# Second routed layer: experts ranked by load, run in pairs of 128 and 64 slots, steps of 1,024 columns

## What is computed

```python
D_MODEL, SEQ, TOP_K = 1024, 256, 2      # N_EXPERTS_2 = 8, D_FF_EXPERT = 3584
def moe_swiglu(x, w_router, w_gate, w_up, w_down):
    logits = (x @ w_router).astype(jnp.float32)
    top_val, top_idx = lax.top_k(logits, TOP_K)
    top_w = jax.nn.softmax(top_val, axis=-1)
    gate = jnp.einsum('bsk,bske->bse', top_w,
                      jax.nn.one_hot(top_idx, N_EXPERTS_2, dtype=jnp.float32)).astype(x.dtype)
    y = jnp.zeros_like(x)
    for e in range(N_EXPERTS_2):
        h = jax.nn.silu(x @ w_gate[e]) * (x @ w_up[e])
        y = y + gate[..., e:e + 1] * (h @ w_down[e])
    return y
```

## Time and profile before

| what | value |
|---|---|
| time, median of 3 runs (range) | 2262.71 us (2261.13 to 2263.49) |
| span of the profiled execution | 2253.2 us |
| TensorE matmul busy | 2128.2 us, 94% |
| TensorE weight load, VectorE, ScalarE busy | 76%, 69%, 57% |
| read from HBM over the span | 595.15 MB |

### The profile page before, as it was taken

The page is one execution under the profiler, slowest core; times in us unless marked ns, Lnnn a source line. Parts: engine busy times, 40 slices in busy tenths (PEclk is TensorE's granted clock), DMA queues, the critical chain, the costliest instruction groups (busy, mean ns, idle before and its releaser), DMA issues. The chain is left out here.

```text
span 2253.2 us, 33106 instructions
## 1 busy us (share of the span) xinstructions
PE 2128.2 (94%) x12230; PEld 1708.1 (76%) x12230; DVE 1550.7 (69%) x2214; ACT 1274.0 (57%) x1674; POOL 196.4 (9%) x148
## 2 busy tenths in 40 slices
PE   8998999998988989999998899999999999999996
PEld 8886884443787779997777688888888888888885
DVE  4557651221555686665367789888888888888887
ACT  4554441111334454443464777787777878777774
POOL 2112100000000113340001010101001010001000
PEclk9998999999989999999999899999999999999999
DMA  8640649999552245658212899999999999999994
GB/s 264 197 150 1 196 158 393 417 416 415 176 178 94 85 153 163 203 163 215 80 40 99 301 369 367 373 367 374 370 375 367 375 377 368 374 369 371 368 396 177
DMA packets 293952, 602.56 MB, mean 267 GB/s; under 512 B 17835, under 2 KB 123711, under 8 KB 285520
## 3 DMA queue, kind: packets, MB, share of 16 engines
q1 hardware_dynamic: 285392, 571.56, 70.2%
q0 software_dynamic: 8448, 29.49, 4.1%
HBM read 595.15 MB, written 5.83 MB: 267 GB/s over the span
## 5 line engine op out<-in xcount | busy, mean ns | idle before, releaser
L2139 ACT ACTIVATE arena_rounded<-ring 128x1024 fp32r<-128x1024 f32 x452 | 470.9, 1061 | 114.8 <-DMA ring<-in_moe_w_up_dram 67.0
L2856 DVE TENSOR_TENSOR ring_rounded<-ring,arena_rounded 128x1024 fp32r<-128x1024 f32 x452 | 525.0, 1218 | 13.1 <-ACT arena_rounded L2139 11.6
L1210 PE MATMUL psF<-arena_rounded 128*128 128x512 f32 x896 | 357.6, 399 | 1.6 <-ACT arena_rounded L2161 1.6
L1212 PE MATMUL psF<-arena_rounded 128*128 128x512 f32 x896 | 354.2, 395 | 0.0
L1211 PE MATMUL psF<-ring_rounded,arena_rounded 128*128 128x512 f32 x896 | 352.9, 394 | 0.0
L2413 DVE TENSOR_TENSOR ring_rounded<-ring,ring_rounded 128x2048 fp32r<-128x2048 f32 (+1 forms) x68 | 147.1, 2165 | 157.0 <-ACT ring_rounded L1965 156.8
L1212 PEld LDWEIGHTS psF<-arena_rounded 128*128 128x128 f32 x896 | 168.5, 188 | 39.2
L1210 PEld LDWEIGHTS psF<-arena_rounded 128*128 128x128 f32 x896 | 168.8, 188 | 38.9 <-ACT arena_rounded L2161 1.8
L1211 PEld LDWEIGHTS psF<-ring_rounded,arena_rounded 128*128 128x128 f32 x896 | 168.7, 188 | 37.8
L1211 PE MATMUL psB<-ring_rounded,PT_rounded 128*128 128x512 f32 x448 | 177.6, 396 | 0.0
L1965 ACT ACTIVATE ring_rounded<-ring 128x2048 fp32r<-128x2048 f32 (+1 forms) x71 | 128.6, 1813 | 84.7 <-PE psF L1212 62.7
(11 more groups left out here) (485 smaller groups left out, 4625.8 us busy)
## 6 DMA issues: line engine op xcount, KB each, us to landing
ring<-in_moe_w_gate_dram SPq DMA_DIRECT2D x224, 512.0 KB, 5.8
ring<-in_moe_w_up_dram SPq DMA_DIRECT2D x224, 512.0 KB, 5.7
ring<-in_moe_w_down_dram SPq DMA_DIRECT2D x224, 512.0 KB, 5.5
ring<-in_w_dram SPq DMA_DIRECT2D x48, 1024.0 KB, 16.7
arena<-in_w_dram SPq DMA_DIRECT2D x16, 1024.0 KB, 18.9
ring<-in_w_in_dram SPq DMA_DIRECT2D x14, 1024.0 KB, 5.3
ring<-in_ff_w_gate_dram SPq DMA_DIRECT2D x11, 1024.0 KB, 7.2
ring<-in_ff_w_up_dram SPq DMA_DIRECT2D x11, 1024.0 KB, 9.7
```

Of the source, the lines that this page charges most:

```text
L1210: mm(bank, x1, w1, start=start, stop=False, skip_group_check=open_groups)
L1212: return mm(bank, x2, w1, start=False, stop=stop, skip_group_check=open_groups)
L2139: ap_(half_slot(slot, w_hi).bitcast(R32), half_slot(slot, raw_halves), ACT.Copy).then_inc(q["high"], 1)
L2856: V.tensor_tensor(half_slot(slot, low_halves).bitcast(R32), half_slot(slot, raw_halves), half_slot(slot, w_hi), ALU.subtract).then_inc(q[" ...
```

## The change

The second routed layer is rewritten; the rest of the program stays.

1. **Order and slots.** The counts of all experts are summed on TensorE ("totals2"), and `sort_experts` on VectorE (some 26 small instructions and two of 128 x 896) ranks them: expert 0 stays first with 128 slots; the four with most tokens of the others take positions 1, 3, 5, 7 with 128 slots (`BIG`), the three with the fewest take positions 2, 4, 6 with 64 slots (`FEW`). SyncE reads the expert's number for a position from SBUF. If an expert had more tokens than slots, the old form of the layer would run as a second round.
2. **Steps.** Each expert has 4 steps: three of 1,024 columns (24 pieces of 512 KB: 8 gate, 8 up, 8 down) and one of 512 (12 pieces). Position 0 runs alone, then the pairs (1, 2), (3, 4), (5, 6) take turns step by step, then position 7 runs alone.
3. **The 128-slot experts** keep the products by halves. A step of 1,024 columns has three PSUM banks; the first four pieces of up are gone through twice, once for each half of the columns, the second time after the SiLU has freed a bank. Down pieces are loaded, rounded and subtracted two at a time (1 MB, 128 x 2,048).
4. **The 64-slot experts** multiply in plain float32 straight from the ring, with no high and low: a stationary block of 128 x 64, the two halves of the piece's columns into partitions 0 to 63 and 64 to 127 of one bank.
5. **Rows.** Gate and up pieces of a 1,024-column step have rows of 4 KB; a down load reads 8 KB per partition that lie together (16 KB rows of four, two at a time).
6. **The rest.** The rows of all seven later experts are numbered in one go; GpSimd brings and stores rows in a written-out order, 64 rows for the small ones. Semaphores of the old form get base values (`layer.wait`, `base`), so that the old form can still run after the new one.

The core of the diff ("..." marks what is left out):

```diff
+BIG = (0, 1, 3, 5, 7)
+FEW = 64
+HALF_SLOTS = 2 * RING
...
+class Step:
+
+
+    def __init__(self, t, pos, s, alone):
+        self.t, self.pos, self.s, self.alone = t, pos, s, alone
+        self.big, self.wide = pos in BIG, s < 3
+        self.first, self.last = s == 0, s == 3
+        self.base = 1024 * s
+        self.pieces = 8 if self.wide else 4
+        self.halves = 2 if self.big and self.wide else 1
+
...
+        for group in ((0,), (1, 2), (3, 4), (5, 6), (7,)):
+            for s in range(4):
+                for pos in group:
+                    self.steps.append(Step(len(self.steps), pos, s, len(group) == 1))
+        n = len(self.steps)
+        self.at, self.pieces, self.loads = {}, [], []
+        for t in range(n + 1):
+            for part, u in (("gate", t), ("up", t), ("down", t - 1)):
+                if not 0 <= u < n:
+                    continue
+                for j in range(self.steps[u].pieces):
+                    idx = len(self.pieces)
+                    self.at[u, part, j] = idx
+                    self.pieces.append(self.steps[u].big)
+                    if part != "down" or j % 2 == 0:
+                        self.loads.append((idx, u, part, j, 2 if part == "down" else 1))
+        self.big_no = list(itertools.accumulate(int(b) for b in self.pieces))
+        self.landed, self.count = {}, [0] * HALF_SLOTS
+        for idx, _, _, _, n_ in self.loads:
+            slot = idx % HALF_SLOTS
...
+            def load_sorted(layer):
...
+                for idx, t, part, j, n in order.loads:
+                    st = order.steps[t]
+                    if st.pos not in expert:
+                        if len(expert) == 1:
+                            sp.wait_ge(experts_sorted, 1)
+                        expert[st.pos] = nc.sync.value_load(expert_no[0:1, st.pos:st.pos + 1], min_val=0, max_val=E2 - 1)
...
+                    if idx >= HALF_SLOTS:
+                        sp.wait_ge(piece_used, idx + n - HALF_SLOTS)
...
+                    if part == "down":
+                        c = st.base // 512
+                        if st.wide or st.big:
+                            src = fours[e, c + j // 4, :, j % 4:j % 4 + 2, :]
+                        else:
+                            src = twos[e, c, j // 2, :, :, :]
+                        src = src.rearrange("e p f n -> p (e f) n")
+                    elif st.wide:
+                        src = (gates if part == "gate" else ups)[e, j // 2, :, j % 2, st.base:st.base + 1024]
+                        src = src.rearrange("e p n -> p e n")
+                    else:
+                        src = (gates if part == "gate" else ups)[e, j, :, :, st.base:st.base + 512]
+                        src = src.rearrange("e p a n -> p (e a) n")
...
+                def few_product(st, bank, part, j):
+
+                    w = few_piece(st.t, part, j, 1 if st.wide else 2)
+                    for a in range(1 if st.wide else 2):
+                        k = j if st.wide else 2 * j + a
+                        for b in range(2):
+                            n = 512 if st.wide else 256
+                            ins = mm(bank[FEW * b:FEW * b + FEW, 0:n], few_T[:, k, :], w[:, a, n * b:n * b + n],
+                                     start=(k == 0), stop=(k == KT - 1))
+                    ins.then_inc(piece_used, 1)
+
...
+                def gate(st):
+                    if st.first:
+                        if st.big:
+                            pe.wait_ge(x_low, order.halved_x[st.pos + 1])
+                        else:
+                            pe.wait_ge(x_high, order.turned_x[st.pos + 1])
...
+                        X = many_banks(st)
+                        hi, lo = big_piece(st.t, "gate", j, 1 if st.wide else 2)
+                        for b in range(2):
+                            ins = many_product(X[b], j, hi, lo, 0, cols[b]) if st.wide else \
+                                many_product(X[0], 2 * j + b, hi, lo, b, cols[0])
+                        ins.then_inc(piece_used, 1)
...
+                    for j in range(4):
+                        hi, lo = big_piece(st.t, "up", j)
+                        many_product(X[2], j, hi, lo, 0, cols[0])
+                    pe.wait_ge(half_silu, order.halves[st.t] + 1)
+                    for j in range(4):
+                        hi, lo = (piece(order.at[st.t, "up", j], m).rearrange("p (a n) -> p a n", a=1) for m in (w_hi, low_halves))
+                        many_product(X[0], j, hi, lo, 0, cols[1]).then_inc(piece_used, 1)
+                    for j in range(4, 8):
+                        hi, lo = big_piece(st.t, "up", j)
+                        many_product(X[2], j, hi, lo, 0, cols[0])
+                        many_product(X[0], j, hi, lo, 0, cols[1]).then_inc(piece_used, 1)
+
...
+                def turn(st):
+                    if not st.big:
+                        pe.wait_ge(half_hidden, order.halves[st.t + 1])
+                        n, every = (512, 4) if st.wide else (256, 2)
+                        for i in range(every):
+                            ins = nc.tensor.transpose(few_G[:, P * i:P * i + P], few_hidden[:, i:n:every], eye)
+                        ins.then_inc(half_turned, 1)
+                        return
+                    X = many_banks(st)
+                    for b in range(st.halves):
+                        pe.wait_ge(half_hidden, order.halves[st.t] + b + 1)
+                        for i in range(4):
+                            ins = nc.tensor.transpose(X[1 + b][:, P * i:P * i + P], many_hidden[:, b, i:512:4], eye)
+                        ins.then_inc(half_turned, 1)
...
+                def down(st):
+                    if st.big:
...
+                    for j in range(st.pieces):
+                        first_, last_ = st.first and j == 0, st.last and j == st.pieces - 1
+                        if st.big:
+                            hi, lo = big_piece(st.t, "down", j)
+                            for c in range(2):
+                                ins = product(Y[c][:, :], many_T[j // 4][0][:, j % 4, :], many_T[j // 4][1][:, j % 4, :],
+                                              hi[:, 0, cols[c]], lo[:, 0, cols[c]], first_, last_)
+                        else:
+                            w, per = few_piece(st.t, "down", j), 4 if st.wide else 2
+                            at = P * (j % per) + FEW * (j // per)
+                            for c in range(2):
+                                ins = mm(few_Y[FEW * c:FEW * c + FEW, :], few_hiddenT[:, at:at + FEW], w[:, 0, cols[c]],
+                                         start=first_, stop=last_)
+                        ins.then_inc(piece_used, 1)
...
+                for t in range(len(steps) + 1):
+                    st = steps[t] if t < len(steps) else None
+                    prev = steps[t - 1] if t else None
...
+                    if st is not None:
+                        gate(st)
+                    if prev is not None:
+                        turn(prev)
+                    if st is not None:
+                        if st.big and st.first and not st.alone:
+                            turn_x(st.pos + 1)
+                        if not st.big and st.last:
+                            turn_x(st.pos + 1)
+                        up(st)
+                    if t == 0:
...
+                    if prev is not None:
+                        down(prev)
...
+                def highs_of(t, part, js):
...
+                            if part == "down" and j % 2:
+                                continue
+                            n = 2 if part == "down" else 1
+                            slot, count = order.landed[idx]
+                            act.wait_ge(piece_in[slot], count)
+                            ap_(pieces_at(idx, n, w_hi).bitcast(R32), pieces_at(idx, n, raw_halves), ACT.Copy).then_inc(piece_high, n)
...
+                for t in range(len(steps) + 1):
+                    st = steps[t] if t < len(steps) else None
+                    prev = steps[t - 1] if t else None
...
+                    if st is not None:
+                        silu(st)
+                    if prev is not None:
+                        turned(prev)
+                    if st is not None:
+                        if st.big and st.first and not st.alone or not st.big and st.last:
+                            save_x(st.pos + 1)
+                        highs_of(t, "up", range(4, 8))
+                    if t >= 2 and steps[t - 2].last and t != order.first_of[7] + 1:
+                        save_y(steps[t - 2])
+                    highs_of(t - 1, "down", range(8))
+                    if t == order.last_of[0]:
+                        save_x(1)
...
+                            dve.wait_ge(piece_high, order.big_no[idx] + n - 1)
+                            V.tensor_tensor(pieces_at(idx, n, low_halves).bitcast(R32), pieces_at(idx, n, raw_halves),
```

(25 more changed lines are left out.)

738 lines of the change are left out of this document (538 added, 200 removed).

## The result

The changed kernel takes 2242.6 us (median of 4 runs, 2240.3 to 2245.9) against 2262.9 of the kernel before beside it: a ratio of 0.992 (95% interval 0.9905 to 0.9934), 20.3 us less. Forecast were 75.8 less and 2187 us, with a range from 2160 to 2235. So it is faster, as forecast, by about a quarter of the size. Its profiled execution has a span of 2240.6 us and stands only 2.0 us under the median of its runs; compared with that of before (2253.2) it shows 12.6 us, not 20.3. What follows explains the difference to the forecast from spans inside one execution.

What follows compares the result with a forecast made beforehand. TensorE bounds the layer before the change, loads narrowly bound the pairs after. Expert 0 124.6, pairs 651.4, last wait 5.8 and expert 7 121.6 make 903.4 against 979.2 us: 75.8 less, 2187 us, range 2160 to 2235.

Steps and rivals of the forecast that it cites:

- edits priced at nothing: Before the pairs: `sort_experts` (7.5 us) at nothing, 5 us if uncovered; the totals' matmuls under the wait for first picks.
- stage A: Expert 0, and gate and up of expert 1's first step; the forecast's terms give 146.9 us.
- the 30.5 us of the forecast: VectorE's work for a 128-slot step of 1,024 columns; nothing for the 64-slot step.
- I take 1.5 us lost per cycle (between 0 and 4): Pairs: loads' loss per cycle with a ring of 12 pieces, 3 in flight; 10.5 cycles, 16 us.
- the ring: Pairs: 12 pieces against 24 large, then 24 small pieces in order of use; 16 us lost in all.
- stage B: The pairs, from the first to the last product of a small expert; the forecast's terms give 657.2 us.
- The rate: Loads in the pairs: 417 GB/s, bounds 390 and 425; 264.2 MB in 633.6 us, plus 11.8 us for rows.
- Expert 7: 119.6 + 2.0: Last lone expert: TensorE's 119.6 us as before, plus 2.0 for the uncovered turn at the end; 121.6 us.
- TensorE and its waits: Rival, pairs: a second uncovered hand-over of 4.4 us per cycle, 42 us more, 2229 us; chance 0.20 (2210 to 2240).
- The loads don't get faster: Rival, pairs: load engines at their limit, 373 GB/s, layer 971 us, time 2255 us; chance 0.06.
- The bound of about 358 GB/s per core: Rival, pairs: HBM side limits loads, pairs 752 us, time about 2287 us; chance 1 in 100.
- Halves one after the other: Rival, 64-slot products: halves don't run side by side, a piece costs 1.71 us, time 2343 us; chance 0.04.

Runs made afterwards that it cites:

- single down pieces: Changed kernel with the large experts' down pieces rounded and subtracted one at a time instead of two: 2212.2 us, ratio 0.9793 to the kernel before.
- all three edits: Changed kernel with by eights, single down pieces and The ends' run's orders, down before turned x in the pairs: 2190.4 us, ratio 0.9704; again 2190.8 us.
- light large products: Changed kernel with two of three matmuls of each large product left out for experts 1, 3 and 5 (output wrong): 2201.3 us, one run.
- The ends' run: Changed kernel with three orders altered outside the pairs' wide cycles (earlier row save, last down pieces before turned rows): 2234.1 us, ratio 0.989; again 2232.1 us.
- by eights: Changed kernel reordered so that 8 large and 8 small pieces alternate in the pairs instead of 24 and 24: 2228.6 us, ratio 0.9869.
- eights and ends: Changed kernel with by eights and The ends' run's orders, down before turned x, down pieces still in twos: 2202.9 us, ratio 0.9751.

## Why the prediction was right in direction and wrong in size

**What held.** In the pairs TensorE alone is no longer the bound: in each small run it now waits for the loads. But the rate there was to be over 400 GB/s, and under 400 was my sign of a wrong forecast; it is 389 over 1,420 to 2,080 us. A small piece costs what the first layer's did: records of two in a line, 16 of them in 3.06 us from first start to last in the time line, and a step's 24 pieces about 22 us. The chain from the landing of the first down pair to TensorE is 4.45 us (forecast 4.4) and is followed by half clock. Loads at 371 GB/s in expert 0 (forecast under 370, as TensorE bounds there). Of the edits priced at nothing, the tokens' 28 matmuls take 3.18 us of TensorE in stage A, within the 5 us that I had allowed for that stage. For the sorting ahead of the layer nothing is shown: the first product starts 3.7 us later than in the one trace of before, but it starts anywhere from 1255.6 to 1264.4 us in the traces of the changed kernel and its forms. VectorE and ScalarE are busy for 34 to 56% of each 100 us in the pairs, less than my 60%; the 30.5 us of the forecast over its own cycle of 62.7 us would have been 49%.

**The term that failed: "I take 1.5 us lost per cycle (between 0 and 4)".** Measured is the difference of the cycles with and without the heavy large run: 66.0 - 61.5 = 4.5 us, above my upper bound. I had counted how far TensorE falls behind (9 pieces), so that 3 would be in flight, and took 3 in 4.1 us for nearly the full rate. The count holds, if the wait and the half clock are in it: 24 x (1.43 - 1.258) = 4.1 us are only 3 pieces, the 5.8 us at the start 4.6 more, and two had landed before. What failed is the step from there to 1.5 us. The landing time isn't a constant 4.1 us: in the slow stretch it was 5.5 to 6.9 us, and three pieces in 5.5 us are 286 GB/s. And slots don't come free evenly every 1.43 us: in the large up SyncE issues nothing for 4.65 us (1757.07 to 1761.72 in the time line; 4.66 with single pieces), more than the 3.8 us that three pieces last at 1.258 (an estimate). The wait at the start counts nearly in full on top: the run with single down pieces takes 2.0 us off it and 2.3 off the cycle, and the 2.2 us left over go with the dip in the large up. Forecast for the ring were 16 us of stage B. With B at 652.9 us in the run of all three edits and 653.4 with light large products, it cost 689.2 - 652.9 = 36.3.

**The rate.** 410 instead of 417 GB/s: 269.1 MB take 656.3 instead of 645.3 us, 11.0 us. With the 20.3 of the ring that is 31.3 of the 32.0 us of stage B. The rate lay inside the bounds that I had (390 to 425); that of the ring was outside of its own, and I let its low value stand because both sides of the comparison were so level that neither seemed to matter.

**The lone experts.** "Expert 7: 119.6 + 2.0" missed 19.1 us, about a third of the whole error. I had followed VectorE's order inside the steady steps, and not ScalarE's at the two joints: a small save behind eight landings (6.14 us), and the double down pieces behind the last turned rows (5.84), each with half clock behind it, and two waits of 1.9 and 2.0 us. The ends' run took 11.4 us of it away by order alone. In expert 0, 8.6 us over, single down pieces recover 3.4 (a gap of 2.48 us before a down becomes 1.74, the 144 matmuls behind it take 34.5 instead of 36.0 us, and the 456 ahead of it 1.1 less); the rest wasn't tried.

**The rivals.** The time lies between those of two rivals, and neither is its cause. *TensorE and its waits* (2229) needed a second uncovered hand-over, which doesn't exist; there is one long wait per cycle, and it acts through the ring. *The loads don't get faster* (2255) is excluded by 410 GB/s with light products and 413 by eights. The bound of about 358 GB/s per core that the Trainium skill gives ("DMA: Bandwidth & Descriptors", section "Where 436 GB/s comes from") doesn't hold for the lone core of these runs, which moved 410 over 500 us. *Halves one after the other* is excluded by the small pieces' records.

**What stays open.** The stage sums of the changed kernel's two profiled executions differ by 5 us, 4.5 of them in stage B, and I haven't found what moves it; it is also why the ends' first run looked small. How the 2.2 us per cycle in the large up divide between the double pass, the turn and the loads in twos isn't shown, since no run changed one of them alone (light large products shorten the double pass as well as the pace), and 5.2 of the 8.6 us in expert 0 have no cause shown.

## What to carry to other kernels

When a change moves the bound from an engine to the loads, the ring must bridge the longest run of pieces that the engine takes more slowly than they land. Every wait at the start of that run counts as time in which slots are held, and so does a stretch at its end in which pieces are used and none is freed. So look at when slots come free, and not only at the mean pace. Mixing slow and fast users of the ring in shorter runs did here (29 us) what a larger ring would have to do, and a ring two pieces smaller cost over 50. An operation that takes two pieces at a time saves little on an engine with slack and puts its full length into the one place where TensorE waits for its first piece.

## What the runs showed of the hardware

TensorE's clock after a wait isn't decided by the wait's length alone. In the run of eights and ends TensorE waited the same time twice, 2.93 and 2.94 us from the last small product's start, after the same work for the 10 us before (the large gate's end, 16 records, a turn, 16 records):

```profile
1489.63 0.63 PE L1418 MATMUL psB<-arena_rounded,PT_rounded 128*128 128x512 f32 x1
1490.06 0.63 PE L1416 MATMUL psB<-arena_rounded,PT_rounded 128*128 128x512 f32 x1
...
1552.50 0.39 PE L1418 MATMUL psB<-arena_rounded,PT_rounded 128*128 128x512 f32 x1
1552.73 0.39 PE L1416 MATMUL psB<-arena_rounded,PT_rounded 128*128 128x512 f32 x1
```

Once the matmuls behind it were 0.43 us apart, once 0.23. In the second run of all three edits that gap is at most 2.5 us, and TensorE had the full clock (1.00) over 1,500 to 2,000 us.

The median time from issue to landing of a 512 KB load was 4.1 us with nothing before it, 5.5 at 332 GB/s and 11.6 at 416: at the full rate it measures the queue, and a low value in a slow stretch says that loads weren't issued.
